# Twelve RMS norms: the inverse root of two columns of token sums, spread over the partitions by TensorE

## The reference

```python
def rmsnorm(x, w):
    xf = x.astype(jnp.float32)
    y = xf * lax.rsqrt(jnp.mean(xf * xf, axis=-1, keepdims=True) + RMS_EPS)
    return (y * w.astype(jnp.float32)).astype(x.dtype)

h = rmsnorm(x, mix_pre_norm[l])                           # norm 5 (3, 7, 9, 10 are alike)
x = x + rmsnorm(merged @ w_out[l], mix_post_norm[l])      # norm 6 (2, 4 and 8 are alike)
```

## Time and profile before

| | us |
|---|---|
| median of 3 runs (lowest, highest) | 1958.48 (1957.59, 1959.07) |
| the profiled execution | 1962.91 |
| its span, first to last instruction | 1961.10 |
| mean granted TensorE clock, share of full speed | 0.883 |

### The profile page before, as it was taken

One profiled execution on the slowest core, in us unless ns is written; L12 is line 12 of the kernel. 1 busy time (PEld: TensorE's weight loads), 2 busy tenths in 40 slices (PEclk: granted clock), 3 DMA queues, 4 the chain that ended last, 5 costly groups with the idle time before them and its releaser, 6 DMA issues.

```text
span 1961.1 us, 24549 instructions
## 1 busy us (share of the span) xinstructions
PE 1520.7 (78%) x10333; PEld 1026.8 (52%) x10333; DVE 712.4 (36%) x1129; ACT 598.4 (31%) x1008; POOL 5.3 (0%) x8
## 2 busy tenths in 40 slices
PE   5999785655665656665556668999989999898997
PEld 3887631111211111111111128999988999797897
DVE  4457500000000000000000018768767884568564
ACT  5434410000000000000000025775755664455453
POOL 0000100000000000000000000000000000000000
PEclk8999798788787787887887888999998999899899
DMA  9555679999999999999999993433453454343230
GB/s 400 212 232 223 258 311 429 428 428 429 429 428 428 428 429 428 429 430 428 428 428 429 427 427 144 172 123 136 161 213 129 176 201 164 137 172 118 92 124 22
DMA packets 48606, 570.24 MB, mean 291 GB/s; under 512 B 4624, under 2 KB 10896, under 8 KB 12048
## 3 DMA queue, kind: packets, MB, share of 16 engines
q1 hardware_dynamic: 43072, 559.96, 69.7%
q10 hardware_dynamic: 5456, 9.15, 1.4%
HBM read 564.89 MB, written 4.19 MB: 290 GB/s over the span
## 4 chain that ended last, share of the span: by engine, by line
PE 50%; DMA 40%; DVE 6%; ACT 3%; issue 1%; SPq 0%; ACTq 0%; DVEq 0%
PE bank L1442 49%; DMA ring<-in_w_down 13%; DMA ring<-in_w_up 13%; DMA ring<-in_w_gate 13%; DMA ring<-in_w_ada 1%; ACT work L1787 1%; ACT weights_high_rounded L1787 1%; DVE rstd L2006 1%; DVE h_normed L2010 1%; DVE ring_rounded L2057 1%; DVE h_normed_rounded L2000 0%; DVE work L1281 0%; DVE small L1275 0%; DVE small L1261 0%; DVE work L1268 0%
## 5 line engine op out<-in xcount | busy, mean ns | idle before, releaser
L1442 PE MATMUL bank<-ring,work 128*32 128x512 f32 x3008 | 485.8, 779 | 310.5 <-DMA ring<-in_w_up 126.3
L1787 ACT ACTIVATE work<-bank 128x256 f32<-128x256 f32 (+3 forms) x243 | 110.5, 467 | 1107.9 <-PE bank L1442 782.6
L1442 PEld LDWEIGHTS bank<-ring,work 128*32 128x32 f32 x3008 | 93.6, 127 | 669.9 <-DMA ring<-in_w_up 206.9
L2057 DVE TENSOR_TENSOR ring_rounded<-ring,weights_high_rounded 128x1024 fp32r<-128x1024 f32 x208 | 252.8, 1222 | 136.6 <-ACT weights_high_rounded L1787 136.3
L1787 ACT ACTIVATE weights_high_rounded<-ring 128x1024 fp32r<-128x1024 f32 x244 | 255.3, 1051 | 25.9 <-PE bank L1442 25.8
L2263 DVE TENSOR_TENSOR work<-work,bank 128x512 f32<-128x512 f32 x16 | 16.5, 1029 | 592.1 <-PE bank L1442 592.1
L1442 PE MATMUL bank<-h_high_rounded,weights_high_rounded 128*128 128x256 f32 x1296 | 205.0, 297 | 18.2 <-ACT h_high_rounded L1787 16.7
L1442 PEld LDWEIGHTS bank<-h_high_rounded,weights_high_rounded 128*128 128x128 f32 x1296 | 174.8, 195 | 36.0 <-issue 23.6
L1442 PE MATMUL bank<-h_high_rounded,ring_rounded 128*128 128x256 f32 x1296 | 181.5, 282 | 6.3 <-DVE ring_rounded L2057 3.9
L1442 PE MATMUL bank<-h_normed_rounded,weights_high_rounded 128*128 128x256 f32 x1296 | 181.3, 284 | 0.0
L1442 PEld LDWEIGHTS bank<-h_high_rounded,ring_rounded 128*128 128x128 f32 x1296 | 165.8, 193 | 7.2 <-DVE ring_rounded L2057 4.3
(11 more groups left out here) (231 smaller groups left out, 1141.1 us busy)
## 6 DMA issues: line engine op xcount, KB each, us to landing
ring<-in_w_down SPq DMA_DIRECT2D x64, 2048.0 KB, 16.2
ring<-in_w_gate SPq DMA_DIRECT2D x63, 2048.0 KB, 16.1
ring<-in_w_up SPq DMA_DIRECT2D x61, 2048.0 KB, 16.4
ring<-in_dense SPq DMA_DIRECT2D x60, 2048.0 KB, 8.2
ring<-in_w_ada SPq DMA_DIRECT2D x12, 2048.0 KB, 12.7
work<-in_w_up SPq DMA_DIRECT2D x3, 1024.0 KB, 14.2
bias_diagonals<-work SPq DMA_DIRECT2D x2, 1536.0 KB, 9.5
ring<-in_dense SPq DMA_DIRECT2D x2, 1024.0 KB, 17.2
```

What stands on the lines that cost most here:

```text
L1442: return nc.tensor.matmul(o, lhsT, rhs, start=start, stop=stop)
L1787: return nc.scalar.activation(o, i, f, **kw)
L2057: v.tensor_tensor(as_r(w), w, w_high[:, buffer, :], ALU.subtract).then_inc(s.w_low, 1)
```

## The change

The roles of the two operands in the column sum are exchanged: the squares (a 128x128 piece, one half of the tokens) are the stationary operand and one column of ones is the moving one. The result is one column of 128 token sums, with the tokens on the partitions; two columns for 256 tokens, 16 products of one column for a norm in place of 8 products of 256 columns. The root and the reciprocal then work on 128x2 values, in a small SBUF tile `ROOT`. A new step, `spread_rstd(i)`, brings the result back to all partitions: two products with `ROOT`'s column, repeated 128 times, as stationary operand and the identity matrix as moving one, into a PSUM bank `rstd(i)`. DVE's multiplications read this bank in place of `RS`.

`spread_rstd` is called right behind the last column sum of each norm; for norms 0 and 1 both spreads stand behind both sums and ahead of the other three quarters of the product, and PE waits there for `norm_inverted` 1 and 2 and for the identity matrix (`consts_in`). Three semaphores of tables at the start become one (`tables_ready`), which DVE waits for with the value 3 where it had waited for one of them. `RS` stays for another use.

```diff
--- before.py
+++ after.py
@@ -197,7 +197,7 @@
-        sm = sb("small", [P, 844])
+        sm = sb("small", [P, 868])
@@ -217,6 +217,14 @@
+        def norm_bank(i):
+
+            return B[{0: 6, 4: 3}.get(i, 7)]
+
+        def rstd(i):
+
+            return B[{0: 2, 1: 3, 4: 2}.get(i, 6)][:, 0:SEQ]
@@ -272,6 +280,7 @@
         ROOT_WARM, EPS_COL = small(812, 12), small(824, 1)
+        ROOT = small(844, 24).rearrange("p (i t) -> p i t", t=TT)
...
@@ -495,6 +504,7 @@
             column_sum(6, KT - 1)
+            spread_rstd(6)
             column_sums(7)
...
@@ -719,7 +730,7 @@
-            dve.wait_ge(s.a_exp, 1)
+            dve.wait_ge(s.tables_ready, 3)
...
@@ -1480,19 +1493,29 @@
-            def column_sum(i, k, bank=7):
+            def column_sum(i, k):
 
                 pe.wait_ge(s.norm_squared, KT * i + k + 1)
                 if i > 1 and k == 0:
                     pe.wait_ge(s.norm_root, i)
-                last = mm(B[bank][:, 0:SEQ], ones[:], (HH_plain if i == 1 else SQ)[:, k, :], k == 0, k == KT - 1)
+                sq = HH_plain if i == 1 else SQ
+                for t in range(TT):
+                    last = mm(norm_bank(i)[:, t:t + 1], sq[:, k, t * P:(t + 1) * P], ones[:, 0:1],
+                              k + t == 0, k + t == KT + TT - 2)
                 if k == KT - 1:
                     last.then_inc(s.norm_summed, 1)
 
-            def column_sums(i, bank=7):
+            def spread_rstd(i):
+
+                pe.wait_ge(s.norm_inverted, i + 1)
+                for t in range(TT):
+                    last = mm(rstd(i)[:, t * P:(t + 1) * P], ROOT[:, i, t:t + 1].broadcast_to([P, P]), ident)
+                last.then_inc(s.rstd_spread, 1)
+
+            def column_sums(i):
                 for k in range(KT):
-                    column_sum(i, k, bank)
-
+                    column_sum(i, k)
+                spread_rstd(i)
@@ -1515,8 +1538,12 @@
             ada_block_product(0)
-            column_sums(0, bank=6)
-            column_sums(1)
+            for i in range(2):
+                for k in range(KT):
+                    column_sum(i, k)
+            pe.wait_ge(s.consts_in, 16)
+            spread_rstd(0)
+            spread_rstd(1)
             for b in range(1, 4):
                 ada_block_product(b)
...
@@ -1820,10 +1848,10 @@
-            def root(i, bank=7):
+            def root(i):
 
                 act.wait_ge(s.norm_summed, i + 1)
-                fn(RS[:, i % 2, :], B[bank][:, 0:SEQ], ACT.Sqrt, scale=1.0 / DM, bias=EPS_COL).then_inc(s.norm_root, 1)
+                fn(ROOT[:, i, :], norm_bank(i)[:, 0:TT], ACT.Sqrt, scale=1.0 / DM, bias=EPS_COL).then_inc(s.norm_root, 1)
...
@@ -2003,12 +2031,12 @@
             def norm_invert(i):
 
                 dve.wait_ge(s.norm_root, i + 1)
-                v.reciprocal(RS[:, i % 2, :], RS[:, i % 2, :]).then_inc(s.norm_inverted, 1)
-                dve.wait_ge(s.norm_inverted, i + 1)
+                v.reciprocal(ROOT[:, i, :], ROOT[:, i, :]).then_inc(s.norm_inverted, 1)
+                dve.wait_ge(s.rstd_spread, i + 1)
 
             def times_rstd(i, dst, src, gain, k):
                 return v.scalar_tensor_tensor(out=dst[:, k, :], in0=src[:, k, :], scalar=gain[:, k:k + 1],
-                                              in1=RS[:, i % 2, :], op0=ALU.mult, op1=ALU.mult)
+                                              in1=rstd(i), op0=ALU.mult, op1=ALU.mult)
```

More of the change, by code:

```diff
@@ L103 @@
 xse_ready hid_ready hid_tr hidt_sb selt_ready y_low y_high acc_done act_step params_in ctx_in x_in zeros_ready
-decay_soft toep_stored ramp_ready dmat_ready xi_ready g_silu yc_ready yvar_ready yrstd_ready h2_scaled
+tables_ready toep_stored ramp_ready dmat_ready xi_ready g_silu yc_ready yvar_ready yrstd_ready h2_scaled
 logit_shift aff_exp silu_sb ffn_sb dve_step norm_inverted decay_ready""".split()
@@ L391, in ffn_conved, with tensor_block2 @@
             return tiles(u - 1, 1) if u % 2 else tiles(48 + u // 2, 1)
-        def tensor_block2(pe, mm, dense_unit, column_sum, column_sums):
+        def tensor_block2(pe, mm, dense_unit, column_sum, column_sums, spread_rstd):
             def unit2(unit, act, name=None):
@@ L514, in tensor_block2 @@
             column_sum(8, KT - 1)
+            spread_rstd(8)
         def scalar_block2(act, fn, link, square, squares_of_x, root_table, root, unit_done, weight_high, split_high):
@@ L730, in vector_block2 @@
             last.then_inc(s.cs_ready, 1)
-            dve.wait_ge(s.lam_soft, 1)
+            dve.wait_ge(s.tables_ready, 3)
             link(v.tensor_scalar(LAMC, par("lru_lam"), -1.0, 0.0, ALU.mult, ALU.max))
@@ L927, in load_biases, with tensor_block3 @@
             act.dma_start(BIAS[:, :, P:3 * P], second).then_inc(s.bias_in, 16)
-        def tensor_block3(pe, mm, dense_unit, dense_tokens, column_sum, column_sums):
+        def tensor_block3(pe, mm, dense_unit, dense_tokens, column_sum, column_sums, spread_rstd):
             normed = by_tile(HH), by_tile(as_r(H[:, :, :]))
@@ L1053, in tensor_block3 @@
             column_sum(10, KT - 1)
+            spread_rstd(10)
             def odd(*units):
@@ L1075, in tensor_block3 @@
             column_sum(11, KT - 1)
+            spread_rstd(11)
         def scalar_block3(act, fn, link, squares_of_x, root_table, root, unit_done, weight_high, split_high):
@@ L1661, in _ @@
             column_sum(2, KT - 1)
+            spread_rstd(2)
             column_sums(3)
@@ L1760, in _ @@
             expert(EXPERTS - 1, final=True)
-            column_sums(4, bank=3)
-            tensor_block2(pe, mm, dense_unit, column_sum, column_sums)
-            tensor_block3(pe, mm, dense_unit, dense_tokens, column_sum, column_sums)
+            column_sums(4)
+            tensor_block2(pe, mm, dense_unit, column_sum, column_sums, spread_rstd)
+            tensor_block3(pe, mm, dense_unit, dense_tokens, column_sum, column_sums, spread_rstd)
         @block.scalar
@@ L1838, in _ @@
             link(fn(LT, LT, ACT.Exp, scale=-1.0))
-            fn(LT, LT, ACT.Ln, bias=1.0).then_inc(s.decay_soft, 1)
+            fn(LT, LT, ACT.Ln, bias=1.0).then_inc(s.tables_ready, 1)
             link(fn(LAMT, par("lru_lam"), ACT.Abs))
             link(fn(LAMT, LAMT, ACT.Exp, scale=-1.0))
-            fn(LAMT, LAMT, ACT.Ln, bias=1.0).then_inc(s.lam_soft, 1)
-            fn(NEGA, par("a_log"), ACT.Exp).then_inc(s.a_exp, 1)
+            fn(LAMT, LAMT, ACT.Ln, bias=1.0).then_inc(s.tables_ready, 1)
+            fn(NEGA, par("a_log"), ACT.Exp).then_inc(s.tables_ready, 1)
             act.wait_ge(s.ctx_in, 16)
@@ L1852, in _ @@
             root_table(0)
-            root(0, bank=6)
+            root(0)
             root(1)
@@ L1969, in _ @@
             last.then_inc(s.ffn_sb, 1)
-            root(4, bank=3)
+            root(4)
             for unit in range(AHEAD2):
@@ L2048, in _ @@
             dve.wait_ge(s.params_in, 16)
-            dve.wait_ge(s.decay_soft, 1)
+            dve.wait_ge(s.tables_ready, 1)
             v.scalar_tensor_tensor(out=LG, in0=par("decay"), scalar=0.0, in1=LT, op0=ALU.min,
@@ L2083, in _ @@
                 for half in (slice(0, 4), slice(4, KT)):
-                    v.tensor_tensor(dst[:, half, :], src[:, half, :], spread(RS[:, i, :], 1, 4),
+                    v.tensor_tensor(dst[:, half, :], src[:, half, :], spread(rstd(i), 1, 4),
                                     ALU.mult).then_inc(s.first_normed, 1)
```

4 lines of the change are left out of this document (2 added, 2 removed).

## The result

The changed kernel takes 1978.76 us (median of 4 runs, 1972.29 to 1980.31), the kernel before 1958.78 (4 runs) beside it: ratio 1.0089, 95% interval 1.0072 to 1.0106, some 17.5 us slower by the ratio; the two medians, each of 4 runs, lie 20.0 us apart. The forecast was 1961.9 with a range up to 1966.5, so time and range were both missed. The profiled execution took 1980.31 us (span 1978.5), the one of before 1962.91 (1961.1). In the tables further on two single executions far above all others, one of the run best (4779 us) and one of the kernel before beside it (2505 us), are left out.

What follows compares the result with a forecast made beforehand. Expert weights set the pace from 269 to 1161 us; elsewhere PE or handovers between PE, ACT and DVE. Start +5.4 and norm 2 on -2.0 made +3.4 on 1958.48: 1961.9 us, range 1954.5 to 1966.5.

Steps and rivals of the forecast that it cites:

- Short steps: Each norm's root and reciprocal on 128x2 values: 0.29 and 0.17 us, together 1.76 us less per norm.
- The spread: Two new products on each norm's chain: 0.79 us with handover at 2.4 GHz, 1.3 us at 1.2 GHz.
- Rival (d): The spread's repeated operand loads at half the pace, 0.45 us more in each of ten norms: 1966.5; chance 0.07.
- The chain of a norm: Last column sum to first multiplication: 0.97 us shorter at the full clock, 0.46 at the half.
- The clock: One-column sums leave the clock down or let it fall: norms 3, 5, 7, 9 lose 3.2 us, router 0.9.
- (a): Rival: narrow passes hold the clock up and raise it; together -12.7 us, 1945.8; chance 0.06.
- (b): Rival: narrow passes hold the clock where it is up but don't raise it; 1955; chance 0.11.
- The router's term: The router's 9 fast passes become slow: 0.9 us lost.
- The start: Norms 0 and 1 and three product quarters: norm 1's sums slow, ACT's copy +5.4 us later; bounds +3.2 and +8.2.
- Rival (c): The start is not on the chain, say because first dense weights come later: 1956.5; chance 0.09.
- From norm 2 on: Norms 2 to 11: gains of 6.9 us against losses of 0.8 (interleaved sums), 3.2 and 0.9: -2.0 us.
- The base: Profiled execution taken as 4.4 us above the median from its own overhead; +3.4 added to median 1958.48.

Runs made afterwards that it cites:

- best: Changed kernel with small at 876 floats, 128 columns in all column sums, both start reciprocals ahead of the multiplications: 1953.32 us, 0.9969 of the kernel before.
- oldstart: As layout, but norms 0 and 1 in the old form (wide sums, 256-column root and reciprocal, no spread): 1964.25 us, 1.0014 of the kernel before.
- cols: As layout, but each column sum multiplies by all 128 columns of ones, not one: 1959.44 us, 0.9988 of the kernel before.
- layout: Changed kernel with small back at 844 floats and the roots in a tile allocated last, older tiles in old places: 1971.90 us, 1.0047 of the kernel before.
- mixed: As oldstart, but the sums of norms 3, 5, 7 and 9 multiply by 128 columns of ones: 1957.70 us, 0.9977 of the kernel before.

## Why the prediction failed, step by step

- **Short steps, right.** In the changed kernel, root of 128x2: 261 ns in the mean of 12 (0.29 foretold); reciprocal 165 ns (0.17); multiplication 479.
- **The spread, right.** 0.71 us at the full clock, 1.22 at the half (0.79 and 1.3 with the handover). Rival (d), a doubled load of the repeated operand, is out.
- **The chain of a norm, right.** From the end of the last square to the first multiplication the trace of before has 3.08 us at norms 2, 6 and 8, and oldstart and the changed kernel 1.96: 1.12 less (0.97 foretold); at norm 11 3.14 and 2.02. At norm 10 only 0.52 is gained: behind the interleaved one-column sums the clock is recorded at 0.50 from 1861.0, just ahead of its spread at 1861.35, which took 1.22, not the 0.7 to 0.8 I had named; in cols, with 128 columns, it stayed at 1.00 and the gain was 1.03. Norms 3, 5, 7 and 9 changed by +0.98, +0.08, +0.33 and +0.27 in the changed kernel (foretold, with the slow spread: +0.94, -0.26, +0.24, +0.44). Norm 4 had no clock term in the forecast; its 32 sums took 5.82 us in the changed kernel's trace, where the clock fell during them, against 3.72 before and 3.73 in layout.
- **The clock, right in kind.** One-column passes neither raise nor hold it: they were busy throughout at 0.50 from 226.5 to 233.4, and in layout the clock was up in norm 0's sums (0.98) and down in norm 1's (0.50) without a pause between them. Layout and cols differ in nothing but columns. That excludes rivals (a) and (b) for the one-column form. The Trainium skill, TensorE: Matmul & The Clock Gate, section What's actually happening, lets the gate follow how busy PE has been; these rows do not agree, since PE's busy share was full in norm 1's sums in both layout (0.50) and cols (1.00). The router's term was 0.9 and measured 7.01 - 5.87 = 1.1.
- **The start, mis-sized.** The step was "Sums of norm 0 begin at 15.9 at the full clock (16 to 20)". In the profiled execution of before the clock had just come up there; in that of the changed kernel it had not, and one-column passes did not raise it. Norm 0's sums took 7.0 us, not 3.7, and the whole came to 8.5 us instead of 5.4, beyond the bound of 8.2. Where they had the full clock (layout) the slip was 5.7 and the first dense product came at 44.15, 0.15 past the 43 to 44 foretold. Timed, the start costs 6.5 us, so 5.4 was mis-sized by about 1 and the larger error lies in the next step. The three quarters took 7.15 us against 7.4 foretold. Rival (c) is out.
- **Missing: the placement.** "If the dense layers behind start with the clock where it was, nothing else moves" was the step that failed. I read the line with 868 as an allocation and gave it no cost, no bound and no rival. In the up layer, at a clock of 1.00 in both traces, the products still lost 0.64 us in each 33. It costs 0.42% to 0.59%, 8 to 12 us, by these figures the largest part of the loss.
- **From norm 2 on, -2.0 foretold.** With the moved tiles and the start taken out, oldstart is at 1.0014 (1.0001 to 1.0027), +2.8 us. The steps in its trace add up to what was foretold: norms 2, 6, 8 and 11 at -1.12 each, norm 10 -0.52, norms 3, 5, 7 and 9 together +1.55, router +1.1, and from the forecast, not measured, norm 4's root -0.18 and the interleaved sums +0.8, that is -1.7. So some 2 to 7 us by the interval are not in this list; its profiled execution ended 0.8 us ahead of that of before, its timed ones did not. By oldstart against mixed the one-column blocks, their slow spreads and the slow router behind them cost 7 us, where my terms held 3.2 + 0.9 + 4 x 0.5 = 6.1. The remainder stays open.
- **The base.** I subtracted 4.4 us as the profiled execution's own overhead. Over the 84 later runs of the kernel before the medians are 1961.4 to 1962.3, near its profiled 1962.91, and other kernels' profiled executions lie among their timed ones. The first three runs were at the low end, and the sum should have stood on the profiled time: 1966.3. The upper end 1967 of the forecast's own range fits neither base: with the start's bound of +8.2 and the -2.0 it is 1964.7 on the median and 1969.1 on the profiled time. The measured 1978.76 lies above all of these.

The ledger in the order of the runs, each step with an uncertainty of some 0.2%: changed kernel to layout -0.42% (tiles), layout to oldstart -0.33% (start), oldstart to mixed -0.37% (clock in the four blocks), and mixed stands at -0.23%: what the idea of the change is worth in norms 2 to 11 without its three side effects.

## What to carry to other kernels

A tile that grows moves all that is allocated behind it, and matrix products can lose 2% of their pace by that alone; put new tiles last, or time the kernel before with only the allocation changed. A product with fewer columns that takes as long as a wide one saves nothing and can cost the clock: when a reduction may be done with one column or with 128 at the same number of passes, the wide one was 11.6 us faster here (cols against layout). A clock read in one execution at a place where it has just risen is no term but a range: take both levels for the bound.

## What the runs showed of the hardware that I had not expected

- The pace of products whose operands are streamed and loaded from SBUF depends on where the tiles lie relative to each other: 113.5 to 119.5 ns from start to start for one pair of tiles when one of them moves by 32 bytes, 113.5 again when all tiles move by 96. One execution repeats the same few intervals: in the kernel before 100 of 172 of that pair's products are 113 ns after the one ahead.
- A block of 128x1 products kept the granted clock at 0.50 for 7 us at a full busy share (226.50 to 233.40), and norm 1's passes, at 0.50 with one column, ran at 1.00 with 128 (20.60 to 24.10 in cols).
- The granted clock shown ahead of a trace's first clock record is not a reading: 1.00 was shown while the passes were 0.213 us apart.
